# One order of TensorE's work in the attention of a fused trunk step: scores, turn, values against values, turn, scores

## What is computed

```python
# windowed attention ("swa"): 8 query heads, 2 key/value heads of 64, one sink logit per head
s = scale * q @ k.T                     # band mask for latent queries, plus all context keys
p = softmax(concat([s, sink]))[..., :-1]
o = p @ v
# low-rank attention ("mla"): 8 heads, key = 64 of the head + 32 shared rotary dimensions
s = scale * (q_nope @ k_nope.T + q_rope @ k_rope.T)
o = softmax(s) @ v
```

## Time and profile before

| what | value |
|---|---|
| median of 3 runs | 1251.12 us (1247.42 to 1253.12) |
| the profiled execution's own time | 1250.76 us |
| its span, first to last instruction | 1248.9 us |
| mean granted TensorE clock | 0.956 of full |
| TensorE matmul busy | 1154.1 us (92%) |
| TensorE weight loads busy | 1047.4 us (84%) |
| VectorE, ScalarE, GpSimd busy | 444.4, 430.8, 541.0 us |
| the attention's steps | about 834.7 to 907.7 us of the span |

### The profile page before, as it was taken

How to read it: one execution, slowest core, us unless ns; L and a number is a source line. 1 busy time by engine, 2 the same in 40 slices (tenths; PEclk the granted TensorE clock), 3 DMA queues, 4 the chain that set the end, 5 groups by cost and what they waited for, 6 DMA issues and landing times.

```text
span 1248.9 us, 17436 instructions
## 1 busy us (share of the span) xinstructions
PE 1154.1 (92%) x7238; PEld 1047.4 (84%) x7238; DVE 444.4 (36%) x822; ACT 430.8 (34%) x658; POOL 541.0 (43%) x414
## 2 busy tenths in 40 slices
PE   5699998999988999999999989778998999999997
PEld 3399898977767999999999869565597999999996
DVE  4523899215766311111111230428655101111112
ACT  0442422452343423322222242447615333323222
POOL 0344588330015364554455524113043565565662
PEclk9599999989999999999999979889998999999998
DMA  9743323345234666655566642042025444434331
GB/s 311 252 127 104 101 68 102 118 136 189 82 85 138 180 188 185 187 169 170 164 202 184 173 158 68 17 119 68 1 68 135 111 125 135 121 105 117 116 117 51
DMA packets 242940, 163.84 MB, mean 131 GB/s; under 512 B 20214, under 2 KB 241453, under 8 KB 242862
## 3 DMA queue, kind: packets, MB, share of 16 engines
q1 hardware_dynamic: 214880, 135.74, 37.5%
q10 hardware_dynamic: 27982, 26.99, 6.9%
HBM read 159.81 MB, written 2.90 MB: 130 GB/s over the span
## 4 chain that ended last, share of the span: by engine, by line
PE 74%; DVE 12%; ACT 5%; DMA 3%; POOL 3%; issue 2%; ACTq 0%; SPq 0%; DVEq 0%
PE banks L410 19%; PE banks L412 18%; PE banks L411 18%; POOL w_lo L1014 3%; PE banks L484 3%; ACT w_hi L1038 2%; DVE ht L1467 1%; PE banks L450 1%; PE banks L452 1%; PE banks L451 1%; DMA raw<-in_ada_w 1%; DVE h_lo L1458 1%; DVE Qd L1635 1%; DMA raw<-in_w_in_even 1%; DVE Kd L1635 1%
## 5 line engine op out<-in xcount | busy, mean ns | idle before, releaser
L1014 POOL TENSOR_TENSOR w_lo<-raw,w_hi 128x512 fp32r<-128x512 f32 (+2 forms) x410 | 540.8, 1349 | 685.3 <-ACT w_hi L1038 685.3
L410 PE MATMUL banks<-h_hi,w_hi 128*128 128x384 f32 x1152 | 394.6, 343 | 24.4 <-DVE h_lo L1458 16.7
L411 PE MATMUL banks<-h_lo,w_hi 128*128 128x384 f32 x1152 | 388.8, 338 | 0.0
L412 PE MATMUL banks<-h_hi,w_lo 128*128 128x384 f32 x1152 | 388.7, 337 | 0.0
L1038 ACT ACTIVATE w_hi<-raw 128x2048 fp32r<-128x2048 f32 (+4 forms) x115 | 193.4, 1682 | 206.3 <-PE banks L412 157.8
L410 PEld LDWEIGHTS banks<-h_hi,w_hi 128*128 128x128 f32 x1152 | 218.5, 190 | 37.9 <-issue 30.7
L411 PEld LDWEIGHTS banks<-h_lo,w_hi 128*128 128x128 f32 x1152 | 218.7, 190 | 0.7
L412 PEld LDWEIGHTS banks<-h_hi,w_lo 128*128 128x128 f32 x1152 | 218.3, 190 | 0.6
L1510 DVE TENSOR_TENSOR uf<-sa,banks 128x384 f32<-128x384 f32 x44 | 24.4, 554 | 330.2 <-PE banks L412 324.2
L410 PE MATMUL banks<-u_hi,w_hi 128*128 128x384 f32 x352 | 118.8, 338 | 0.9 <-POOL w_lo L1014 0.9
L412 PE MATMUL banks<-u_hi,w_lo 128*128 128x384 f32 x352 | 117.7, 334 | 0.0
(11 more groups left out here) (348 smaller groups left out, 1288.2 us busy)
## 6 DMA issues: line engine op xcount, KB each, us to landing
raw<-in_ffn_w SPq DMA_DIRECT2D x88, 512.0 KB, 5.2
raw<-in_ada_w SPq DMA_DIRECT2D x28, 1024.0 KB, 5.9
raw<-in_ffn_w SPq DMA_DIRECT2D x32, 704.0 KB, 4.6
vada_raw<-in_ada_w ACTq DMA_DIRECT2D x20, 1024.0 KB, 6.7
raw<-in_w_in_even SPq DMA_DIRECT2D x18, 1024.0 KB, 5.2
raw<-in_w_out_even SPq DMA_DIRECT2D x4, 1024.0 KB, 5.7
raw<-in_w_in_odd SPq DMA_DIRECT2D x3, 1024.0 KB, 7.3
raw<-in_w_in_odd SPq DMA_DIRECT2D x8, 256.0 KB, 4.4
```

What stands on the lines that cost most here:

```text
L410: pe.matmul(out, s_hi, m_hi, start=first and j == 0, stop=False)
L411: pe.matmul(out, s_hi, m_lo, start=False, stop=False)
L412: mm = pe.matmul(out, s_lo, m_hi, start=False, stop=last and j == len(terms) - 1)
L1014: ins = pool.tensor_tensor(w_lo[s % SPLIT][:, at:to], raw[u % RAW][:, at:to], w_hi[s % SPLIT][:, at:to].bitcast(F32), ALU.subtract)
```

## The change

In the loop of L934 the three calls stand in the opposite order: first the values of job n-3, then the turn of job n-2, then the scores of job n. Nothing is added or taken away, and the orders of the other engines stay.

```diff
             for n in range(len(jobs) + VALUE_LAG):
+                if n >= VALUE_LAG:
+                    values(n - VALUE_LAG, jobs[n - VALUE_LAG])
+                if 0 <= n - TURN_LAG < len(jobs):
+                    turned(n - TURN_LAG, jobs[n - TURN_LAG])
                 if n < len(jobs):
                     scores(n, jobs[n])
-                if 0 <= n - TURN_LAG < len(jobs):
-                    turned(n - TURN_LAG, jobs[n - TURN_LAG])
-                if n >= VALUE_LAG:
-                    values(n - VALUE_LAG, jobs[n - VALUE_LAG])
```

## The result

The changed kernel takes **1310.5 us** (1298.4 to 1315.5, four runs) against 1252.1 for the kernel before beside it: a ratio of 1.044, interval 1.035 to 1.054. The forecast was 1282.5 us with a range of 1273 to 1294. The direction and the wait came as described; the size did not, and the time lies 5.5 us above where the first rival put it (1305). The profiled execution is the fastest of the four, 1298.36 us with a span of 1296.4.

What follows compares the result with a forecast made beforehand. TensorE was taken as the bound. Added to 1251.12 us, +29.3 from scores(2) to scores(19), +2.2 at the start and -0.1 at the end make +31.4: 1282.5 us, range 1273 to 1294.

Steps and rivals of the forecast that it cites:

- the wait: TensorE's turn waits for VectorE's scaling in nearly every attention step, some 1.3 us in mla and 1.6 in swa.
- the first rival: Clock stays at the lower level all through the attention, transposes not counting as busy: 22 us more, 1305 us; chance 0.10.
- the sum: Attention steps from scores(2) to scores(19): plain steps of 4.57 us (swa) and 4.66 (mla), with splits and clock 88.1 us.
- the forecast's 104: Length of the whole attention in the changed kernel: about 104 us in place of 73.
- The start: Before scores(2), the turn of job 0 now stands ahead of them and delays them: +2.2 us.
- the splits: GpSimd's weight splits in steps 3 and 5 slow VectorE's scaling and bias: 2.4 us each, 4.8 in all.
- the term of the clock: Attention steps 2, 3, 4 and 6 run at the lower clock, 1.3 us each: 5.2 us.
- the end: From scores(19) to the output projection: 9.93 us for 10.07, the 6.07 behind turn(18) unchanged: -0.1 us.
- behind the attention nothing changes: After the attention no time is added; the output projection's weights are split during the attention in both orders.
- The price of a slow step: An attention step at the lower clock costs 1.3 us more, from slower scores and some 0.4 for a turn of six.
- The second rival: Values first close the output tile earlier and VectorE's waits shrink: at most 1.0 us won, 1250 us; chance 0.05.

Runs made afterwards that it cites:

- experiment 8: Changed kernel with nine transposes on constants ahead of each wait of the turn for the scaling, as throw-away fillers: 1284.9 us, ratio 1.025.
- 9: Changed kernel with five throw-away matmuls on constants ahead of each wait of the turn for the scaling: 1285.6 us, ratio 1.027.
- 4: Changed kernel with VectorE's two parts exchanged, scaling of job n-1 before the maxima of job n: 1270.7 us, ratio 1.015.
- 6: Kernel before with only the turn moved ahead of the scores, values still last (turn, scores, values): 1305.2 us, ratio 1.042.
- 10: Changed kernel with both lags one longer on all engines (turn of job n-3, values of job n-4): 1262.9 us, ratio 1.009.
- experiment 1: The changed kernel measured again with no edit: 1312.35 us, ratio 1.048.
- experiment 2: Changed kernel with the scores moved ahead of the turn, so values, scores, turn: 1271.5 us, ratio 1.016.
- 7: Changed kernel with nine throw-away matmuls on constants ahead of each wait of the turn for the scaling: 1293.4 us, ratio 1.032.
- 11: Kernel before, order kept, with filler matmuls only where TensorE waited in its first attention steps: 1252.7 us, ratio 0.9996.

## Why the prediction was right and wrong

**The wait was right.** `p_ready` comes behind the scores, and with the turn ahead of the next scores only the values cover it. Plain steps measured 4.68 us in mla and 4.59 in swa (881.38 to 885.97 in the changed kernel) for the 4.66 and 4.57 of the sum, with waits of 1.31 and 1.69 for 1.3 and 1.6. With the waits filled, the whole attention measured 104.8 and 104.4 us (experiments 8 and 9) for the forecast's 104; they had fewer slow steps than the four that I counted. Experiments 4, 6 and 10 show the cause from three sides: VectorE's order, the turn's place, and the lag.

**The start and the splits were right.** From the first scores to scores(2) it took 6.47 us for 4.10 before, +2.4 for the +2.2 of the sum. Step 3 took 7.95 us where the plain step at the lower clock takes 6.24, and step 5 8.39 where the plain one takes 4.59 and its turn ran 0.67 slower; 1.7 and 3.1 make the 4.8 that stood in the sum.

**The step that failed is the term of the clock.** I counted four steps at the lower level, 5.2 us, took the end at -0.1, and said that behind the attention nothing changes. In the profiled execution 13 of the 18 scores ran wholly or in part at the lower level. From scores(2) at 836.22 to scores(19) at 938.22 it took 102.0 us for the 88.1 of the sum: 3.2 too many in the swa steps and 10.7 in the mla steps, where I had counted no slow step. From there to the output projection it was 14.8 for 9.9. With the 0.2 of the start that is 19.0 us more than forecast within the attention, and 2.2 more behind it; the attention's start, 5.0 us earlier, hides part of this in the total. Nearly all of it is clock. In experiment 1, whose mla steps from job 13 on are at 6.8 us throughout, the attention is 22.5 us longer than the forecast's 104.4 (73.0 + 31.4).

Two smaller terms were mis-sized as well. The price of a slow step was too low: a plain swa step takes 6.24 us at the lower level and 4.59 at the upper, 1.65 apart for my 1.3, and a mla step 6.81 and 4.68. I had taken the 0.87 of the earlier trace rows for the whole turn of four blocks; it is what the chain counts of it behind the scores, and the timeline of the kernel before has that turn at 840.88 with 1.01 us to the next start. A turn of six takes 1.54 us for 0.87, so 0.67 more and not 0.4. And the end was not unchanged behind turn(18): in the new order each of the last values pieces stands right behind its own turn and waits 0.96 us for the copy. At full clock this drain takes 6.81 us (experiment 2, 920.01 to 926.82, where these pieces follow each other in the same order) for the 6.07 of the sum, 0.7 more.

Two readings led to the count of four. From one window of 4 us at full clock with TensorE busy for 3.05 of them I concluded that steps busy for 63 to 72% would stay up. The changed kernel was busy for 11.02 of 16.00 us at 914 to 930 and then fell, with no wait longer than 1.31 us in between. The steps before 930 differ in nothing from each other, so a stretch at full clock in one profile says little about the next. And against the rival I held that slowed pieces fill the step and so bring the clock back. They do fill it: 53.33 of 60.00 us in experiment 1, 89%. The clock stayed at 0.50 all the same. In the first profile it did come back, at about 913 us, behind slow steps of much the same kind:

```profile
904.00:912.00 8.00, 6.94 (x27) 3.49 (x27) 2.73 (x7) 2.68 (x7) 0.00 (x0) 0.50 0.00 1
```

So the runs show that the unfilled waits are what costs the clock here: filled, it stays at 1.00 in the mla steps (experiments 7 to 9). They do not show what decides at which step it falls or comes back; experiment 2 is idle for 0.96 us in each mla step and keeps it. How many steps would run slow could not have been read from the rows of the kernel before; the range should have been wider upwards.

**The rivals.** The first, clock low all through, was given 0.10 and its price of 22 us above the forecast is near the 28 that came. Its mechanism was the right one as to place, but not by the way told: it was the share of matmuls without transposes that should have let the clock down. By the rule of the Trainium skill weighed there ("TensorE: Matmul & The Clock Gate", Part 4 on the PE-mode transpose) transposes as fillers would not have helped; experiment 8 says that they do, at 1.00 for 50 us, so the measurement decides against the rule here. Another place of the same page of the Trainium skill fits what happened: its section on a second failure mode, PSUM-queue depth-cycling, tells of a kernel whose TensorE idles briefly between groups of matmuls so often that the clock goes back and forth between its two levels. The trace agrees for the changed kernel, with idles of 1.31 us at each 4.68 and a clock that falls and comes back; experiment 2, with 0.96 at each 4.33, kept the upper level. The second rival, not slower, did not come; ScalarE waited for the values once before and once after.

## What to carry to other kernels

In a software pipeline that is written out by hand on several engines, measure for each wait the time from the question to the answer on the other engine (here 2.07 us), and add up what the asking engine does in between; a reordering that looks free is paid for by the amount in which this cover falls short, in every step. Then price TensorE's clock as part of the same change: a short wait that recurs in each step of a stage bound by TensorE can cost nearly as much again through the clock (here some 27 us, experiment 1 against 8, beside a forecast of 31), and a list of waits does not show it, since it turns up as longer matmuls. If it is in doubt, fill the wait with throw-away matmuls once: the difference is the clock's share, as long as the fillers end before the wait does (experiments 8 and 9; in 7 and 11 they ran over and cost time of their own).

## What the hardware showed that I had not expected

- At the lower level the clock did not recover in 60 us of steps in which TensorE was busy for 89%, idle for 0.64 us in each plain 6.81 (experiment 1); in another execution of the same kernel it came back among such steps.
- Idles of 0.96 us in each 4.33 us step left the clock at 1.00 (experiment 2, 880 to 910 us); with idles of 1.31 in each 4.68 it fell.
- Transposes of fp32 on constants, 1.20 us in each 4.68 us step, held the clock at 1.00 as well as matmuls did (1284.9 and 1285.6 us).
- The changed kernel's four runs lie between 1298 and 1315 us, in step with their mean clocks of 0.933 to 0.914.
- A low clock at the end of the attention is carried on: the first 15 matmuls of the output projection took 0.32 us each for 0.17.
